# State-space stage of an encoder kernel: four tiles of states ahead of the outputs, and five moved steps

## The reference

```
u   = rmsnorm(h, norm_mix[1])
bu  = einsum(b_bar, u);  xs = associative_scan(lam_bar, bu)      # complex, 128 groups x 64 states
y   = real(einsum(c, xs)) + d * u;  y = gelu(y)
h   = h + y * sigmoid(y @ w_glu + b_glu)
h   = h + conv_ffn(rmsnorm(h, norm_ffn[1]))
```

## Time and profile before

| | us |
|---|---|
| median of 3 runs | 2058.82 (2058.51 to 2060.6) |
| profiled execution, its own time | 2061.25 |
| its span | 2059.5 |
| TensorE busy in the span | 2013.6 |
| VectorE busy | 1587.4 |
| ScalarE busy | 1127.9 |
| GpSimd busy | 574.4 |

### The profile page before, as it was taken

One profiled execution on the slowest core, in us unless ns is written; L12 is line 12 of the kernel. 1 busy time (PEld: TensorE's weight loads), 2 busy tenths in 40 slices (PEclk: granted clock), 3 DMA queues, 4 the chain that ended last, 5 costly groups with the idle time before them and its releaser, 6 DMA issues.

```text
span 2059.5 us, 40427 instructions
## 1 busy us (share of the span) xinstructions
PE 2013.6 (98%) x12936; PEld 1761.9 (86%) x12936; DVE 1587.4 (77%) x2212; ACT 1127.9 (55%) x1653; POOL 574.4 (28%) x725
## 2 busy tenths in 40 slices
PE   7999999999999999999999889999999999999997
PEld 6888888888888888888888788888888888888886
DVE  7977668888788888878888887788888888865554
ACT  6654455456666566655555435666665666544443
POOL 8999012950000000027666681200000000001110
PEclk9999999999999999999999999999999999999998
DMA  6555435556666555557777995655555555566664
GB/s 236 164 184 173 134 123 164 189 188 207 211 216 201 192 185 193 183 168 235 238 230 237 306 245 166 197 194 189 188 186 191 186 191 185 188 183 191 188 188 130
DMA packets 147446, 398.71 MB, mean 194 GB/s; under 512 B 23344, under 2 KB 48560, under 8 KB 147392
## 3 DMA queue, kind: packets, MB, share of 16 engines
q1 hardware_dynamic: 126752, 379.30, 58.2%
q10 hardware_dynamic: 20640, 18.75, 2.8%
HBM read 377.02 MB, written 18.87 MB: 192 GB/s over the span
## 4 chain that ended last, share of the span: by engine, by line
PE 87%; POOL 7%; DVE 3%; DMA 1%; issue 1%; ACT 1%; ACTq 0%; SPq 0%; DVEq 0%; POOLq 0%
PE bank L380 50%; PE bank L379 25%; PE bank L376 3%; PE bank L377 1%; PE bank L2016 1%; PE bank L2018 1%; PE bank L2017 1%; DMA uu<-yg 1%; PE bank L2046 1%; DVE lo L358 1%; POOL nt L704 1%; POOL nt L700 0%; POOL nt L703 0%; POOL nt L701 0%; POOL nt L702 0%
## 5 line engine op out<-in xcount | busy, mean ns | idle before, releaser
L358 DVE TENSOR_TENSOR lo<-raw,hi 128x1024 fp32r<-128x1024 f32 x698 | 890.9, 1283 | 194.5 <-ACT hi L351 181.5
L351 ACT ACTIVATE hi<-raw 128x1024 fp32r<-128x1024 f32 x698 | 734.2, 1057 | 405.5 <-PE bank L380 336.2
L380 PE MATMUL bank<-aa,hi 128*128 128x512 f32 x2558 | 894.9, 392 | 0.0
L380 PE MATMUL bank<-xx,hi 128*128 128x512 f32 x2236 | 783.9, 392 | 0.0
L379 PE MATMUL bank<-aa,lo 128*128 128x256 f32 x2558 | 716.5, 280 | 0.0
L379 PE MATMUL bank<-xx,lo 128*128 128x256 f32 x2236 | 627.3, 281 | 1.2 <-DVE lo L358 0.7
L380 PEld LDWEIGHTS bank<-aa,hi 128*128 128x128 f32 x2558 | 480.4, 188 | 100.4
L380 PEld LDWEIGHTS bank<-xx,hi 128*128 128x128 f32 x2236 | 419.8, 188 | 86.9
L379 PEld LDWEIGHTS bank<-aa,lo 128*128 128x128 f32 x2558 | 481.5, 188 | 6.3 <-DVE lo L358 0.3
L379 PEld LDWEIGHTS bank<-xx,lo 128*128 128x128 f32 x2236 | 421.2, 188 | 8.5 <-DVE lo L358 1.3
L389 ACT ACTIVATE lowt<-bank 128x256 f32<-128x256 f32 x212 | 81.0, 382 | 220.1 <-PE bank L380 213.5
(11 more groups left out here) (363 smaller groups left out, 1923.7 us busy)
## 6 DMA issues: line engine op xcount, KB each, us to landing
raw<-in_up SPq DMA_DIRECT2D x344, 512.0 KB, 3.3
raw<-in_down SPq DMA_DIRECT2D x160, 448.0 KB, 3.5
raw<-in_w_in SPq DMA_DIRECT2D x98, 512.0 KB, 3.6
raw<-in_w_out SPq DMA_DIRECT2D x32, 512.0 KB, 3.7
raw<-in_down SPq DMA_DIRECT2D x32, 512.0 KB, 4.3
raw<-in_glu SPq DMA_DIRECT2D x32, 512.0 KB, 3.9
s_c<-cp ACTq DMA_DIRECT2D x16, 256.0 KB, 3.2
s_p<-ut ACTq DMA_DIRECT2D x32, 128.0 KB, 5.3
```

The source lines that it names most:

```text
L351: A.activation(hi[:, s, :], raw[:, s, :], ACT.Copy).then_inc(hi_done, 1)
L358: V.tensor_tensor(lo[:, s, :], raw[:, s, :], hi[:, s, :].bitcast(f32), SUB).then_inc(lo_done, 1)
L380: last = TE.matmul(bank[:, :], hi[:, s, w], x2(k)[:, :, :], start=False, stop=k == total - 1)
```

## The change

- TensorE's order becomes S0 S1 S2 S3 | S4 O0 S5 O1 S6 O2 S7 O3 | ... | S12 O8 S13 O9 S14 O10 S15 O11 | O12 O13 O14 O15, `glu_part(0, 0, 8)`. The counts on `yg_pair` and `u_or_new` go up by one to suit, and ScalarE makes its copy for S4 ahead of those for the outputs (`for_states(4)`, then `for_outputs` of tiles 0 to 3).
- VectorE runs `scan(1)` before `rotate_in(2)` instead of behind it.
- The reciprocal is computed twice: first into a PSUM bank (`rr5_first`), which VectorE's two halves of quarter 0 read, and between the two halves into `rr5`, which releases GpSimd.
- GpSimd scales quarter 2 and does the last `add_skip` after its second tile in the loop instead of before the first.
- VectorE squares channel tile 15, and TensorE adds it to the sum with four further matmuls (eight passes); the four over the other 15 tiles no longer wait for it.
- `gelu_low(0)` moves from VectorE's loop (tile 11) to behind `last_states`.
- The four weight fetches move into SyncE's loop, behind the loads of tiles 7, 9, 11 and 13. ScalarE's last `store_t` moves from its step 1 to its step 3.

```diff
@@ sync
-            for j in range(2, 4):
-                fetch(B_GLU, 4, 0, j, w[j, :, :], BW)
-            for j in range(2):
-                fetch(B_GLU, 4, 1, j, w[4 + j, :, :], BW)
+                if kt in (7, 9):
+                    j = (kt - 3) // 2
+                    fetch(B_GLU, 4, 0, j, w[j, :, :], BW)
+                if kt in (11, 13):
+                    j = (kt - 11) // 2
+                    fetch(B_GLU, 4, 1, j, w[4 + j, :, :], BW)
@@ gpsimd
-                if kt == KT - 1:
+                if kt == KT - 2:
                     ins.then_inc(ssq_ready, 1)
...
-            tile_squares(KT - 1)
...
-            for q in (1, 2):
+            def scaled_inputs(q):
...
-            add_skip(KT - 1)
+            scaled_inputs(1)
             for kt in range(KT - 1):
...
+                if kt == 1:
+                    scaled_inputs(2)
+                    add_skip(KT - 1)
@@ scalar
-            for kt in range(1, 4):
+            for_states(4)
+            for kt in range(4):
                 for_outputs(kt)
-            for_states(4)
...
-                if kt == 1:
+                if kt == 3:
                     store_t(KT // 2 - 1, 1)
@@ vector
+            v.wait_ge(tile_read, Q_DN0 + KT)
+            V.tensor_tensor(rstd[:, :], h[:, KT - 1, :], h[:, KT - 1, :], MUL).then_inc(sq_new, 1)
...
-            V.reciprocal(rr5, sqt_root[:, 0:C5]).then_inc(rr5_new, 1)
-            v.wait_ge(rr5_new, 1)
+            chain(V.reciprocal(rr5_first, sqt_root[:, 0:C5]))
...
-            scaled(0, 0, 2)
-            scaled(0, 2, 4)
+            scaled(0, 0, 2, rr5_first)
+            V.reciprocal(rr5, sqt_root[:, 0:C5]).then_inc(rr5_new, 1)
+            scaled(0, 2, 4, rr5_first)
+            v.wait_ge(rr5_new, 1)
...
-                if kt == 0:
+                if kt < 2:
                     scan(kt)
                 if kt + 1 < KT:
                     rotate_in(kt + 1)
-                if kt > 0:
+                if kt >= 2:
                     scan(kt)
...
-                if kt == 11:
-                    gelu_low(0)
             last_states()
+            gelu_low(0)
@@ tensor
+            p.wait_ge(sq_new, 5)
+            for j in range(T5):
+                last = TE.matmul(pb[5][:, 0:C5], steps..., rstd..., start=False, stop=j == T5 - 1)
             last.then_inc(norm_sum, 1)
...
-            chunk_outputs(0, 0)
             with p.Fori(1, KT // 4) as i:
                 for j in range(4):
                     chunk_states(i, j)
-                    chunk_outputs(i if j == 3 else i - 1, (j + 1) % 4)
+                    chunk_outputs(i - 1, j)
...
+            chunk_outputs(KT // 4 - 1, 0)
             chunk_outputs(KT // 4 - 1, 1)
-            p.wait_ge(q_new, KT - 1)
-            glu_part(0, 0, 4)
             chunk_outputs(KT // 4 - 1, 2)
             chunk_outputs(KT // 4 - 1, 3)
-            glu_part(0, 4, 8).then_inc(block_used, 1)
+            p.wait_ge(q_new, KT - 1)
+            glu_part(0, 0, 8).then_inc(block_used, 1)
```

More of the change, by code:

```diff
@@ L255, in hybrid_encoder @@
         states = pb[2:6]
-        rr5 = rstd[:, 0:C5]
+        rr5, rr5_first = rstd[:, 0:C5], pb[1][:, 0:C5]
         def move_y(eng, x, m):
@@ L612, in _ @@
                 load_c(kt)
-            for j in range(2, 4):
-                fetch(B_GLU, 4, 0, j, w[j, :, :], BW)
-            for j in range(2):
-                fetch(B_GLU, 4, 1, j, w[4 + j, :, :], BW)
-            sp.wait_ge(yg_pair, 1 + KT // 2)
+                if kt in (7, 9):
[4 more added lines that the diff above has]
+                    fetch(B_GLU, 4, 1, j, w[4 + j, :, :], BW)
+            sp.wait_ge(yg_pair, 2 + KT // 2)
             for m in range(2, 4):
@@ L1176, in ffn @@
                     down_and_store(KT // 2 - 1, 1)
-                    A.activation(root_t[0:1, 0:1], ones[0:1, 0:1], ACT.Sqrt).then_inc(yg_pair, 1)
+                    A.activation(root_t[0:1, 0:1], ones[0:1, 0:1], ACT.Sqrt).then_inc(yg_pair, 2)
                     gained(KT // 2 - 1, 1)
@@ L1295, in move_part @@
             def move_part(x, ms):
-                a.wait_ge(yg_pair, 1 + Y_PARTS[x][1] // 2)
+                a.wait_ge(yg_pair, 2 + Y_PARTS[x][1] // 2)
                 for m in ms:
@@ L1350, in _ @@
                     for x in (kt + 1, kt + 2):
-                        if x <= KT - 4:
+                        if x < KT - 4:
                             for_outputs(x)
@@ L1838, in _, with scaled @@
             v.wait_ge(norm_root, 3)
-            V.reciprocal(rr5, sqt_root[:, 0:C5]).then_inc(rr5_new, 1)
-            v.wait_ge(rr5_new, 1)
-            def scaled(q, k0, k1):
+            chain(V.reciprocal(rr5_first, sqt_root[:, 0:C5]))
+            def scaled(q, k0, k1, factor=rr5):
                 for x in range(2 * q + k0 // 2, 2 * q + k1 // 2):
@@ L1845, in scaled @@
                 x = uu[:, q, :, k0:k1, :]
-                V.tensor_tensor(x, x, rr5.unsqueeze(1).unsqueeze(1).broadcast_to([P, 4, k1 - k0, C5]),
+                V.tensor_tensor(x, x, factor.unsqueeze(1).unsqueeze(1).broadcast_to([P, 4, k1 - k0, C5]),
                                 MUL).then_inc(uk_new, 1)
@@ L2230, in _ @@
             for j in range(T5):
+                TE.matmul(pb[5][:, 0:C5], steps[:, j, :, :, :].rearrange("p w q r -> p (w q r)"),
+                          ssq[:, :].rearrange("p (c j) -> p j c", j=T5)[:, j], start=j == 0, stop=False)
+            p.wait_ge(sq_new, 5)
+            for j in range(T5):
                 last = TE.matmul(pb[5][:, 0:C5], steps[:, j, :, :, :].rearrange("p w q r -> p (w q r)"),
-                                 ssq[:, :].rearrange("p (c j) -> p j c", j=T5)[:, j], start=j == 0, stop=j == T5 - 1)
+                                 rstd[:, :].rearrange("p (c j) -> p j c", j=T5)[:, j], start=False, stop=j == T5 - 1)
             last.then_inc(norm_sum, 1)
@@ L2256, in chunk_outputs @@
                 p.wait_ge(t_full[j], 16 * i + 16)
-                if o == 0 and not (isinstance(i, int) and kt < 4):
-                    p.wait_ge(yg_pair, 2 * i + j // 2)
+                if o == 0:
+                    p.wait_ge(yg_pair, 2 * i + j // 2 + 1)
                 if not isinstance(i, int):
-                    p.wait_ge(u_or_new, kt)
+                    p.wait_ge(u_or_new, kt + 1)
                     p.sem_inc(pe_turn, 1)
```

## The result

In 16 runs of each kernel, interleaved, the changed kernel takes 2063.3 us at the median (2061.95 to 2065.5) and the kernel before 2058.85 (2057.89 to 2060.87). The ratio is 1.0020, 95% interval 1.0013 to 1.0027: slower by some 4.45 us. The forecast was 2058.1 with a range from 2053.4 to 2061.8; the measured time lies above it. The profiled execution after has an own time of 2064.81 and a span of 2062.8, so the two profiled executions differ by 3.56 us. Its stage begins earlier in the span: the last residual of the FFN starts at 1164.94, against 1165.55 before.

The account below looks back on a forecast made before the run. The prediction took S4's weight load, then GpSimd in the loop, then ScalarE's DMA wait in the tail as bounds. 0 ahead, +1.65 loop and -2.35 tail gave -0.7: from 2058.82 to 2058.1 us, range 2053.4 to 2061.8.

Parts of the forecast that it names:

- Ahead of the loop, 0: Before the loop: the edits' gains all end in S4's wait for its load, so this part was priced at 0.
- the 3 us of gains: Square, scaling and early scan ahead of the loop: together some 3 us, to GpSimd's first tiles.
- The order, +1.65: In the loop: GpSimd's tile 2 starts at 1188.25, released by O0, and its last tile ends 1.65 us later.
- E: The end of GpSimd's work on tile 14, its last in the loop; 1230.64 us in the kernel before.
- The fetches, 0: Fetches in SyncE's loop: the queue is full but falls little behind, so `p_op` loads land in time; cost 0.
- a landing allowance of 8.6 to 9.1 us: In the loop: time left for a `p_op` load to land, 9.1 us, or 8.6 with a fetch in front.
- the loop waits for its loads: Rival in the loop: fetches raise the landing to 10.2 us, costing 4.8 over three rounds: 2062.9; chance 0.10.
- The tail, -2.35: From GpSimd's last tile to the GLU: ScalarE's 7.35 us wait goes, TensorE becomes late; step 14 at E + 12.6.
- The 1.25 us stall: In the tail, between O14's start and O15's end: a TensorE stall without a shown releaser, kept in the forecast.
- The sum: Whole kernel: 0 ahead of the loop, +1.65 in the loop, -2.35 in the tail, together -0.7 us.

Follow-up runs that it names:

- e10: The kernel before with only the edits ahead of the loop (ScalarE's late `store_t` stays in as well): 2060.18 us against 2059.26.
- e1: The changed kernel with its four weight fetches back behind SyncE's last load: 2062.91 us against 2059.83 for the kernel before.
- e3: The kernel before with nothing but TensorE's new loop order: 2062.43 us against 2059.83.
- e4: The changed kernel with the fetches later, two behind tile 12 and one each behind 13 and 14: 2059.76 us against 2059.83 for the kernel before.
- e2: The kernel before with nothing but the four fetches moved into SyncE's loop: 2056.14 us against 2059.83.
- e5: The changed kernel with TensorE's loop order of before and its counts and copies: 2057.02 us against 2059.57 for the kernel before.
- e12: The changed kernel with the old loop order, e4's late fetches, `gelu_low(0)` in the loop and the split GLU: 2055.72 us against 2059.26 for the kernel before.
- e7: e5 with the `p_op` loads of tiles 4, 5 and 6 each ahead of its own tile's rotation: 2056.51 us against 2059.57 for the kernel before.
- e6: The changed kernel in the old loop order with e4's late fetches: 2055.61 us against 2059.57 for the kernel before.

## Why the prediction was wrong

- **Ahead of the loop, 0: right, but the 3 us of gains reached GpSimd only in part.** The second half of quarter 0 takes 0.63 us instead of 2.84, and the first rotation starts 2.1 us earlier, counted from the stage's start. Then the first scan waits 1.99 us for ScalarE's `lowt`, which the prediction left out: GpSimd's tile 0 starts 0.1 earlier than before and tile 1 1.2 earlier. What is left ends in S4's wait for its load. In VectorE's timeline (line 1851 is 1846 of before, 1878 is 1873):

```profile
1168.25 0.69 DVE L1851 TENSOR_TENSOR uu<-uu,bank 128x512 f32<-128x512 f32 x1
1168.86 0.55 DVE L1912 RECIPROCAL rstd<-sqt_root 128x64 f32<-128x64 f32 x1
1169.32 0.63 DVE L1851 TENSOR_TENSOR uu<-uu,bank 128x512 f32<-128x512 f32 x1
...
1174.41 1.26 DVE L1878 TENSOR_TENSOR_SCAN qq<-lowt,bank 128x256 f32<-128x256 f32 x2 [1.99 <-ACT lowt L1290]
```

  e10 agrees with the 0, within an interval 3.7 us wide. Counted from the stage's start S4 comes 0.5 later than before (1.3 and 1.0 in e1 and e3), which the prediction had no term for; it was not followed up.

- **The order, +1.65: right in place and size.** Tile 2 starts at 1188.44 (predicted 1188.25), released by TensorE. The order alone, with `gelu_low(0)` left in the loop, should cost 1.65 + 0.86 = 2.5 by the prediction's terms; e3 measures E 2.4 later and 2.6 us of time.

- **The fetches, 0: wrong. This is the step that failed.** Its slack was about right: a landing allowance of 8.6 to 9.1 us; TensorE was ready for S11 to S14 8.0, 8.35, 8.8 and 9.9 us after the issue of their loads (S13: 1217.10 - 2.55 - 1205.73). The landing was not: "the queue is full but falls little behind" led to a landing within 8.6, and it became 8.2, 8.9, 11.1 and 12.6. The size that was wrong is the capacity. Demand was put at 399 GB/s and capacity at 385, a figure from a stretch with no moves in flight, while the moves were entered by their bytes, as 40 GB/s. With the moves in flight full queues carry 222 to 247, and over 1200 to 1220 the mean is 280, less than the 319 that loads and moves ask without any fetch. With the new order and no fetch in the loop the longest landing is 7.6 instead of 6.5 (e1, e3), and 9.1 in e4, whose fetches are all issued behind the last `p_op` load; why that one is longer was not followed up. The two fetches issued ahead of S14's load, 1.05 MB, are 3.7 us more at 280 GB/s (an estimate), and its landing became 12.6. The row that would have told stood in the same group: 304 at a share of 1.09, over a stretch with a set of moves in it. The prediction's estimate from the 358 GB/s of the Trainium skill for reads from HBM counts the 40 of the moves among the reads; the reads alone ask 359, so by that figure next to nothing would fall behind.

- **The rival "the loop waits for its loads", 0.10: this one happened.** It said 10.2 us of landing and 2062.9. The waits came, as it said, only because S stands one place earlier: in the old order the same landing of 11.2 meets an allowance one tile (3.3 us) longer, and e2 and e5 wait 0 and 0.44. The price is E at 1237.80, 5.5 later than predicted: GpSimd's two idle times are 5.54. Part of the second is S14's half clock, 1.97 us instead of 1.15, which the rival did not count.

- **The tail, -2.35: mechanism right, size too small.** ScalarE's long wait went, TensorE became the late one. Step 14 stands at E + 11.32 against E + 14.96 before, so -3.64. The 1.25 us stall that the prediction kept did not come. The shortest tails are those of e12 and e2, where the split GLU stays: E + 10.5 and E + 10.6.

- **The sum.** Loop +7.8 from the stage's start (65.1 to 72.9), tail -3.6: +4.1, against 4.45 measured between the medians. (The loop's +7.8 is 0.5 at S4, 1.65 of the order and 5.5 of idle time, and 0.1 of rest.) The predicted +1.65 and -2.35 differ by 6.1 in the loop and 1.3 in the tail.

## What to carry to other kernels

A queue's capacity is to be read in a stretch with the same kinds of transfers as the one that is costed: here full queues moved 365 GB/s without copies between SBUF and SBUF and 222 with them. Two edits that spend the same slack, one by asking for a load earlier and one by putting traffic in front of it, cannot be priced one by one: -3.7 and +2.6 made +2.9. Before one engine is given a lead of one more tile, look which engine bounds the loop: here it was GpSimd, and the new order only made it start later (in e3 its tile 2 starts 22.7 us from the stage's start instead of 18.6).

## What the runs showed of the hardware

- The moves' effect on all queues, above. It shows in the kernel before too: 274 GB/s from 1197.5 to 1204, with moves in flight, and 338 from 1204 to 1209, with none, the queues full in both.
- With full queues SyncE's issue of a single load took up to 2.82 us (`c_op` at 1220.66) against 0.45 to 0.61 in the loop of the kernel before, so what stands behind it is issued late as well.
- TensorE fell back to half clock after the wait of 3.01 us: S14 took 1.97 us as S4 did, not 1.15, and the clock granted was 0.50 from 1223 to 1226, the lower of its two levels. Behind the wait of 2.55, before S13, it stayed at 1.00. In e7 S6 took 1.96 us, behind a wait of 1.83.
- TensorE's idle time without a releaser, 0.9 to 1.8 us in one or two places of the stage, changes place with the kernel: 1.43 in S7 and 1.25 in O15 before, 0.89 in O3 after, 1.76 in e10's O15, 1.67 in e6's S7. What it is was not found.
